# Work of the indexer placed between the products of a projection, and masks ahead of the last rows

## The reference, cut to what matters

```
proj = rmsnorm(x, g_mix) @ w_in              # 1024 x (7*512 + 64 + 8 + 2*1024)
q_d, k_d, q_s, k_s = rope(rmsnorm(.., g))    # per head of 64
q_i, k_i = rope(q_i), rope(k_i)              # no norm
score = einsum(relu(q_i . k_i * 64**-0.5), w_i)      # 8 heads, summed
score = where(causal, score, -inf)
_, idx = top_k(score, 128)                   # only these keys count in the sparse attention
```

## Time and profile before

| what | value |
|---|---|
| median of 3 runs (lowest, highest) | 1251.58 us (1247.12, 1252.23) |
| the profiled execution's own time, its span | 1250.04 us, 1247.9 us |
| busy over the span: TensorE, VectorE, ScalarE, GpSimd | 85%, 36%, 19%, 21% |
| mean granted clock of TensorE | 0.958 |
| `project`, TensorE's first product to the next block's first matmul | 26.12 to 310.57 us |

### The profile page before, as it was taken

How to read it: one execution, slowest core, us unless ns; L and a number is a source line. 1 busy time by engine, 2 the same in 40 slices (tenths; PEclk the granted TensorE clock), 3 DMA queues, 4 the chain that set the end, 5 groups by cost and what they waited for, 6 DMA issues and landing times. The chain is left out here.

```text
span 1247.9 us, 16077 instructions
## 1 busy us (share of the span) xinstructions
PE 1064.7 (85%) x6029; PEld 556.3 (45%) x6029; DVE 454.3 (36%) x1209; ACT 232.7 (19%) x505; POOL 263.3 (21%) x242
## 2 busy tenths in 40 slices
PE   4998889978998999997899969998878877787773
PEld 3554434434454555532256535544434444344442
DVE  4345888885464555322143423211111110111110
ACT  2112212110233333322004311111011011110100
POOL 1011100220453434200200012223222222222111
PEclk9999989989999999898999969999999999999997
DMA  5141122014564533679738549999999999999991
GB/s 182 41 149 33 54 85 93 27 68 164 175 219 134 187 103 102 222 254 332 242 131 343 178 179 401 403 394 392 406 407 405 402 398 401 400 407 405 405 384 40
DMA packets 77120, 304.13 MB, mean 244 GB/s; under 512 B 22402, under 2 KB 22402, under 8 KB 64754
## 3 DMA queue, kind: packets, MB, share of 16 engines
q1 hardware_dynamic: 61618, 273.47, 57.2%
q0 software_dynamic: 9824, 16.98, 4.8%
q10 hardware_dynamic: 5600, 12.65, 2.8%
HBM read 290.03 MB, written 29.66 MB: 256 GB/s over the span
## 5 line engine op out<-in xcount | busy, mean ns | idle before, releaser
L381 PE MATMUL p_z<-k_w,k_xT 128*128 128x512 f32 (+2 forms) x528 | 213.3, 560 | 0.6 <-PEq L148 0.6
L381 PEld LDWEIGHTS p_z<-k_w,k_xT 128*128 128x128 f32 (+1 forms) x528 | 94.8, 193 | 108.2 <-issue 106.7
L793 PE MATMUL a_G<-k_w,k_xT 128*128 128x512 f32 x256 | 130.3, 632 | 2.5 <-ACT k_x L851 2.5
L1938 DVE TENSOR_TENSOR e_den<-e_sig,e_G 128x256 f32<-128x256 f32 x32 | 13.5, 421 | 277.7 <-ACT e_sig L1843 277.7
L888 POOL TENSOR_TENSOR k_x<-k_x 128x512 f32<-128x512 f32 x64 | 80.4, 1269 | 109.8 <-DVE k_side L952 86.7
L1848 ACT ACTIVATE e_y<-e_Y,x_share 64x512 f32<-64x512 f32 x64 | 43.7, 684 | 314.8 <-PE e_Y L1751 305.9
L1969 POOL DMA_INDIRECT out_y_p<-e_y,x_table x32 | 45.0, 1407 | 199.4 <-ACT e_y L1848 154.8
L141 POOL DMA_INDIRECT k_rows<-token_rows,x_table x32 | 31.3, 978 | 187.4 <-PE e_TX L1733 162.1
L793 PEld LDWEIGHTS a_G<-k_w,k_xT 128*128 128x128 f32 x256 | 45.1, 197 | 49.2 <-issue 45.1
L1142 PE MATMUL g_ring<-k_w,k_oT 128*128 128x512 f32 x128 | 60.4, 618 | 0.0
L1943 DVE TENSOR_TENSOR e_a<-e_den,e_U 128x256 f32<-128x256 f32 x32 | 13.5, 421 | 126.5 <-PE e_U L1739 126.5
(11 more groups left out here) (343 smaller groups left out, 1474.5 us busy)
## 6 DMA issues: line engine op xcount, KB each, us to landing
k_w<-in_w_in SPq DMA_DIRECT2D x11, 2048.0 KB, 7.8
k_w<-in_w_gate SPq DMA_DIRECT2D x11, 2048.0 KB
k_w<-in_w_up SPq DMA_DIRECT2D x11, 2048.0 KB
k_xT<-in_w_down SPq DMA_DIRECT2D x11, 2048.0 KB
k_oT<-in_w_gate SPq DMA_DIRECT2D x11, 2048.0 KB
k_side<-in_w_up SPq DMA_DIRECT2D x11, 2048.0 KB
x_page<-in_w_down SPq DMA_DIRECT2D x11, 2048.0 KB
x_merged<-in_w_gate SPq DMA_DIRECT2D x10, 2048.0 KB
```

The lines of the kernel that those rows point to most:

```text
L381: last = nc.tensor.matmul(z[u % 3][0:p, 0:WIDTH[k]], s.xT[:, j, 128 * i:128 * i + p], s.w[:, c % 2, j, 0:WIDTH[k]], start=j == 0, stop=j = ...
L793: last = nc.tensor.matmul(G[u % 2][:], s.xT[:, j, 128 * i:128 * i + 128], s.w[:, q % 2, j, :], start=j == 0, stop=j == KD - 1)
L1938: v.tensor_tensor(den[:], sig[:], G[j][:, 0:HW], ALU.mult).then_inc(chain, 1)
```

## The change

It edits `project` alone. On TensorE, `turns(u)` names which units are turned during the product of u and behind which step: during tile 0 of a kind, the units u-3 and u-2 behind steps 1 and 4; during tiles 1 to 3, unit u-2 behind step 1; during the 8-row unit none. The four page groups stand behind steps 0, 2, 4, 6 of unit 12's product, the last score of the samples' keys and the new keys behind step 0 of unit 13's, and the sample scores behind its step 6. Index scores go three to a unit, behind steps 2, 5 and 7, at the eight 128-row units 15 to 18 and 20 to 23. On ScalarE, copies of turned units and relus come ahead of the unit's gathering and square. On VectorE, everything of the indexer comes ahead of the unit's `sums` and `finish`: the index scores, each followed by a round while `room` lasts, then more rounds (in all 1 for a normed unit with index scores, 4 for another with them, 2 and 5 without, none for an 8-row unit), one round behind `sums` of a normed 128-row unit only, and `masks()` ahead of `sums` and `finish` of the last unit. The samples' weights are made at unit 13 and their scores copied at unit 14.

```diff
+def turns(u):
+
+    i = u % TILES
+    at = [(1, u - 3), (4, u - 2)] if i == 0 else [(1, u - 2)] if i < NT else []
+    return [(j, v) for j, v in at if v >= 0 and is_turned(UNITS[v])]
...
+        PAIR_AT = {2 * n: n for n in range(PAIRS)}
+        EXTRA_AT = (2, 5, 7)
+        prompt_units = [u for u in range(SAMPLE_AT + 2, U) if UNITS[u][1] < NT]
+        extras = {prompt_units[n // 3]: IDX_STEPS[n:n + 3] for n in range(0, len(IDX_STEPS), 3)}
-        extras = {IDX_FROM + 2 + n // 2: IDX_STEPS[n:n + 2] for n in range(0, len(IDX_STEPS), 2)}
...
+            for u in range(U):
+                k, i = UNITS[u]
+                c, p = u // TILES, ROWS[i]
+                if i == 0:
+                    pe.wait_ge(s.w_in[c % 2], 16 * (c // 2 + 1))
+                if u >= 3:
+                    pe.wait_ge(z_free, u - 2)
+                if i == NT and k != "kw":
+                    small_product(nc, z[u % 3], s.xT[:, :, SEQ:TOK], s.w[:, c % 2], KD).then_inc(proj, 1)
+                    continue
+                for j in range(KD):
+                    last = nc.tensor.matmul(z[u % 3][0:p, 0:WIDTH[k]], s.xT[:, j, 128 * i:128 * i + p],
+                                            s.w[:, c % 2, j, 0:WIDTH[k]], start=j == 0, stop=j == KD - 1)
+                    if j == KD - 1:
+                        last.then_inc(proj, 1)
+                    for at, v in turns(u):
+                        if at == j:
+                            turn(v)
+                    if u == SAMPLE_AT and j == 0:
+                        pe.wait_ge(turn_out, turned_before(2 * TILES))
+                        pe.wait_ge(pages_in, 16 * NS * NPAGE)
+                        pe.wait_ge(blk0, 3)
+                    if u == SAMPLE_AT and j in PAIR_AT:
+                        pair(PAIR_AT[j])
+                    if u == SAMPLE_AT + 1 and j == 0:
+                        pair(PAIRS)
+                        new_keys()
+                    if u == SAMPLE_AT + 1 and j == 6:
+                        sample_scores()
+                    if u in extras and j in EXTRA_AT:
+                        index_scores(*extras[u][EXTRA_AT.index(j)])
...
+                for _, v in turns(u):
                     k, i = UNITS[v]
                     p = ROWS[i]
                     act.wait_ge(turned, nt + 1)
...
+                if UNITS[u][1] == NT and UNITS[u][0] != "kw":
+
+                    act.wait_ge(proj, u + 1)
+                    if u >= TILES:
+                        act.wait_ge(y_ready, u - TILES + 1)
+                    for g in range(NB):
+                        nc.scalar.copy(zs[:, 128 * g:128 * g + 128], z[u % 3][32 * g:32 * g + NS, 0:128]).then_inc(zs_ready, 1)
+                    nz += NB
+                    act.wait_ge(zs_ready, nz)
+                if UNITS[u][0] in NORMED:
+                    p = ROWS[UNITS[u][1]]
+                    act.wait_ge(proj, u + 1)
+                    if ns >= 2:
+                        act.wait_ge(ms_ready, ns - 1)
+                    nc.scalar.activation(sq[0:p, ns % 2, :], (z[u % 3][0:p, :] if p > NS else zs[:]), ACT.Square).then_inc(squared, 1)
+                    ns += 1
...
-                sums(u)
-                if k in NORMED and rounds:
-                    take8(rounds.pop(0))
-                finish(u)
+                if u == SAMPLE_AT + 1:
+                    dve.wait_ge(x_ready, PAIRS + 1)
+                    dve.wait_ge(samp, 2)
+                    link(nc.vector.tensor_tensor(wtmp[:], xs[PAIRS % 2][0:64, 8:16], s.c[0:64, C_HM:C_IOTA], ALU.mult))
+                    link(nc.vector.tensor_reduce(wcol[:], wtmp[:], AX.X, ALU.add))
+                    link(nc.vector.tensor_scalar(ew[:], s.c[0:64, C_ET:C_HM], wcol[:], None, ALU.mult))
+                    dve.sem_inc(samp, 1)
+                    dve.sem_inc(x_free, 1)
+                if u == SAMPLE_AT + 2:
+                    dve.wait_ge(x_ready, PAIRS + 2)
+                    link(nc.vector.tensor_copy(score_s[:, 0:PAST], xs[(PAIRS + 1) % 2][0:NS, :]))
+                    dve.sem_inc(x_free, 1)
+                    dve.wait_ge(x_ready, PAIRS + 3)
+                    link(nc.vector.tensor_copy(score_s[:, PAST:PAST + 1], xs[PAIRS % 2][0:NS, 0:1]))
+                    dve.sem_inc(x_free, 1)
+                    rounds += [score_s[:]] * TK_ROUNDS
+                room = 0 if i == NT else (1 if k in NORMED else 4) if u in extras else (2 if k in NORMED else 5)
                 for t, h in extras.get(u, ()):
                     n = 128 * (t + 1)
                     if nx == 0:
@@ -622,26 +662,18 @@
                     nx += 1
                     if h == H - 1:
                         rounds += [score[t - 1][:]] * TK_ROUNDS
-                if u == SAMPLE_AT:
-                    dve.wait_ge(x_ready, PAIRS + 1)
-                    dve.wait_ge(samp, 2)
-                    link(nc.vector.tensor_tensor(wtmp[:], xs[PAIRS % 2][0:64, 8:16], s.c[0:64, C_HM:C_IOTA], ALU.mult))
-                    link(nc.vector.tensor_reduce(wcol[:], wtmp[:], AX.X, ALU.add))
-                    link(nc.vector.tensor_scalar(ew[:], s.c[0:64, C_ET:C_HM], wcol[:], None, ALU.mult))
-                    dve.sem_inc(samp, 1)
-                    dve.sem_inc(x_free, 1)
-                if u == SAMPLE_AT + 1:
-                    dve.wait_ge(x_ready, PAIRS + 2)
-                    link(nc.vector.tensor_copy(score_s[:, 0:PAST], xs[(PAIRS + 1) % 2][0:NS, :]))
-                    dve.sem_inc(x_free, 1)
-                    dve.wait_ge(x_ready, PAIRS + 3)
-                    link(nc.vector.tensor_copy(score_s[:, PAST:PAST + 1], xs[PAIRS % 2][0:NS, 0:1]))
-                    dve.sem_inc(x_free, 1)
-                    rounds += [score_s[:]] * TK_ROUNDS
-                for _ in range(0 if i == NT else 2 if k in NORMED else 5):
-                    if rounds:
+                    if room and rounds:
+                        room -= 1
                         take8(rounds.pop(0))
-            masks()
+                while room and rounds:
+                    room -= 1
+                    take8(rounds.pop(0))
+                if u == U - 1:
+                    masks()
+                sums(u)
+                if k in NORMED and i < NT and rounds:
+                    take8(rounds.pop(0))
+                finish(u)
 
 
 KQV = dict(d=("qd", "kd", "vd"), s=("qs", "ks", "vs"))
```

More of the change, by code:

```diff
@@ L367, in take_bank @@
                 return xs[(ne - 1) % 2]
[L369 to L390, removed]
-                if u == SAMPLE_AT:
[L392 to L406, removed]
-                    bank = take_bank()
[L409 to L413, removed]
-                if u == SAMPLE_AT + 1:
[L415 to L419, removed]
@@ new lines, in pair @@
+            def pair(step):
+                if step < PAIRS:
+                    bank = take_bank()
+                    for n in range(NPAGE):
+                        last = nc.tensor.transpose(bank[:, 128 * n:128 * n + 128],
+                                                   pages_i[:, n, 2 * step:2 * step + 2, :].rearrange("p b d -> p (b d)"), s.ident[:])
+                    last.then_inc(x_ready, 1)
+                b = step - 1
+                if b >= 0:
+                    pe.wait_ge(kTi_ready, b + 1)
+                    last = nc.tensor.matmul(ss[:], qblk[:, 64 * b:64 * b + 64], kTi[:, b % 2, :], start=b == 0, stop=b == PAIRS - 1)
+                    last.then_inc(ss_ready, 1)
@@ new lines, in new_keys, with sample_scores @@
+            def new_keys():
+                bank = take_bank()
+                pe.wait_ge(newk_ready, 2)
+                for b in range(PAIRS):
+                    nc.tensor.matmul(bank[0:64, 0:1], qblk[:, 64 * b:64 * b + 64], newk[:, b:b + 1], start=b == 0, stop=b == PAIRS - 1)
+                pe.wait_ge(wi_ready, TILES)
+                nc.tensor.matmul(bank[0:64, 8:16], s.c[0:NS, C_E:C_ET], wi[0:NS, NT, :], start=True, stop=True).then_inc(x_ready, 1)
+            def sample_scores():
+                pe.wait_ge(samp, 3)
+                bank = take_bank()
+                nc.tensor.matmul(bank[0:NS, :], ew[:], relu_s[:, 0:PAST], start=True, stop=True).then_inc(x_ready, 1)
+                bank = take_bank()
+                nc.tensor.matmul(bank[0:NS, 0:1], ew[:], relu_s[:, PAST:PAST + 1], start=True, stop=True).then_inc(x_ready, 1)
@@ new lines, in index_scores @@
+            def index_scores(t, h):
+                bank, r = take_bank(), 64 * (h % 2)
+                nc.tensor.matmul(bank[:, 0:128 * (t + 1)], qiT[r:r + 64, h // 2, 128 * t:128 * t + 128],
+                                 kiT[r:r + 64, 0:128 * (t + 1)], start=True, stop=True).then_inc(x_ready, 1)
+            for u in range(U):
[29 more added lines that the diff above has]
+                        index_scores(*extras[u][EXTRA_AT.index(j)])
@@ L423, in _ @@
             ns = nt = nx = nz = 0
-            for u in range(U + 2):
+            for u in range(U):
                 if u == 2:
```

## The result

Five runs of the changed kernel took 1255.43 to 1263.94 us, median 1260.43; five of the kernel before 1246.65 to 1252.23, median 1250.88. The recorded ratio of the runs is 1.0069, 95% interval 1.0045 to 1.0094. `project`, from its first product to the next block's first matmul, went from 284.45 us (26.12 to 310.57) to 293.13 us (26.61 to 319.74): +8.7, where the chain followed unit by unit had given -0.6 and the sum taken no change. So the stage alone nearly covers the 9.6 us between the medians.

What follows compares the result with a forecast made beforehand. VectorE was taken to bound the projections until TensorE bounds the last stretch; +0.9 + 10.6 + 2.1 - 13.8 = -0.2, against -0.7 unit by unit, mean -0.5, plus 0.5 for the clock: no change, 1250.8 us, range 1244 to 1257.

Steps and rivals of the forecast that it cites:

- the chain followed unit by unit: VectorE's durations added through `project` to the stage's end: 309.6 against 310.3 us, given as -0.7.
- the sum: Whole stage: +0.9 early part, +10.6 rounds, +2.1 new gap, -13.8 waits gone = -0.2 us; taken as no change.
- TensorE's waits are not the prize: TensorE's waits on VectorE, about 22 us: VectorE is the bound from 122 to 283 us, so they win nothing.
- VectorE's idle end: From 283 to 310 us TensorE is the bound and VectorE busy only 15.4 of 27.3; that idle can be won.
- P11's new wait: Unit 11's product waits 2.5 us for unit 9, whose keys are now turned behind step 1.
- signs of being wrong: VectorE idle over 5 us after 204, or a stage end under 304 or over 316.
- part 3: Three scores at eight units, rounds ahead of sums: relu waits of 3.0 us go, scores cost the same, rounds +10.6.
- One new gap: Before unit 25's sums VectorE waits 2.1 us for TensorE, whose product of unit 25 ends at 203.5.
- only P11 and P16 can reach VectorE: Slow clock after waits: only products of units 11 and 16 delay VectorE; +3.4 us if both pay in full.
- Rival A: New TensorE waits lengthen VectorE's chain at unit 11's product and units 15 to 18: +8.7 us, 1260; chance 0.13.
- The masks cost 1.2 wherever they stand: Stage end on VectorE: masks put ahead of the last copy take 1.2 us, as at their old place.
- the prediction's count: Rounds inside the wait for GpSimd are free: 16 before, 12 now, since an 8-row unit takes none.

Runs made afterwards that it cites:

- the run of the rounds late: Kernel before with one top-k round instead of two behind each 128-row unit of kd and qd; ratio 0.9907, 1240.9 us.
- same-half run: Kernel before with heads reordered so that two neighbouring index scores read the same half of the partitions; ratio 1.0027, stage 288.5 us.
- all-rows run: Changed kernel with each index score contracted over 128 partitions instead of 64, which changes the scores; one run, stage 289.7 us.
- the run of the pairs at the same units: Changed kernel with index scores in neighbouring pairs, four and two in turn at the same eight units; 1266.9 us, ratio 1.0113.

## Why the prediction was wrong

What held: that VectorE sets the pace outside units 20 to 25, that TensorE's waits are not the prize, that VectorE's idle end can be won (by the run of the rounds late), P11's new wait (2.5 forecast, 1.8 measured), the first round after 122, waits for turns in P30, P32, P33 and P35 (0.9 to 4.2 us; the one forecast in P20 was for a bank instead), VectorE free of waits for P38, the rounds' prices to 0.01 us, and the stretch from unit 25's sums to the masks, 103.5 against 104.3. One of its signs of being wrong came true: VectorE ended the stage at 318.2, over 316; and TensorE's last small product started at 309.1, not near 302.

The step that failed is in part 3, "Scores as such cost the same 24 instructions", and with it the price in "One new gap": I took half a pair, 0.53, for a score of tile 3, from rows in which two stood side by side. A lone one takes 1.05, and 0.19 for the change of row mode. The prediction let VectorE set the pace until P23 and had P25 end at 203.5; TensorE set it from P20's third score on, and P25 ended at 211.3. It is most of the +5.0 between units 19 and 25: the same-half run, which lengthens the scores and nothing else, lost 4.4 us in this stretch. The all-rows run shows the two prices. Of the +1.6 before unit 19, 1.3 us are waits for relus of lone scores; that these have the same cause is argued, not shown.

Second, the sentence that "only P11 and P16 can reach VectorE" with a slow clock. P20 can, once TensorE sets the pace there, and it did in three of the four profiled runs that have this wait of 2.5 us and the changed kernel's order of scores, for 3.3 us each; the fourth is the changed kernel's own, whose +8.7 holds none of it. So this step is wrong, but it is no part of the stage measured above. The median lies 5.0 above the profiled run, of which the short remainder of the program in that run accounts for 3.5 against the profile before; how much slow clock the other four runs had, they don't show. Rival A named waits of TensorE and late scores as the mechanism, but the wrong places, and that its 1260 is the median is luck: in the profile its four late units cost 1.3 us of relu waits instead of 4.8, and the product behind P11's wait ran at clock 1.00.

Third, "The masks cost 1.2 wherever they stand": before, SP's two issues had run in their shadow; now they lie open ahead of the next block, and that cost 0.8 us.

A round in an 8-row unit is free, as the prediction's count had it: giving four back took 5.3 us off the stretch from unit 25 on.

## What to carry to other kernels

Before instructions are spread out, look at what ran beside each while they stood together: price a matmul on half the rows from a row where it stands alone. A wait that comes earlier in an in-order queue costs nothing only where another engine sets the pace, and in units with different kinds of work that changes within 30 us (here at P20). When one engine idles in the last part of a stage and is the bound ahead of it, move its work there by count, not the other engine's waits: one number changed in the kernel before brought 0.93%, the whole rearrangement lost 0.69.

## What the runs showed of the hardware

Two matmuls of 64 rows on different halves of the array, neighbours in the queue and in different banks, took 1.06 us together at 512 columns, against 1.91 on one half and 1.05 for one alone. A change between 128 and 64 rows cost 0.19 us each way; transposes of 128 rows between the steps of a product cost only their own 0.43. After an equal wait of 2.5 us of TensorE the granted clock stayed at 1.00 (2.4 GHz) in one run and lay at 0.51 (1.2 GHz) for the score behind it and the next 6 matmuls (5.42 us for 2.84) in another. It was low behind shorter waits too: 0.57 from 117.3 to 121.3 us behind 2.3 us in the changed kernel's P15, 0.63 for 3.6 us behind 1.3 in the run of the pairs at the same units; and it stayed at 1.00 behind 1.8 in the changed kernel's P11.
